# First three experts fixed, the third's gate and up weights loaded early, and the first expert's later passes in short pieces

## What is computed

```python
scores = jax.nn.sigmoid((h @ router_w).astype(jnp.float32))
sel = scores + router_b.astype(jnp.float32)
...                                  # best group of 4 experts, then the 2 best experts in it
hg = jnp.einsum('td,edf->tef', h, w_gate)        # 16 experts, 1024 x 512 each
hu = jnp.einsum('td,edf->tef', h, w_up)          # 1024 x 512 each
act = jax.nn.silu(hg) * hu * gates[..., None].astype(h.dtype)
return jnp.einsum('tef,efd->td', act, w_down)    # 512 x 1024 each
```

## Time and profile before

| | us |
|---|---|
| median of 3 runs | 544.79 (542.86 to 548.34) |
| the profiled execution, whole | 543.45 |
| its span in the trace | 541.7 |
| PE busy in the span | 474.9 (88%) |
| DVE busy | 232.3 (43%) |
| ACT busy | 147.1 (27%) |
| moved by DMA | 164.64 MB, mean 304 GB/s |

### The profile page before, as it was taken

One profiled execution on the slowest core, in us unless ns is written; L12 is line 12 of the kernel. 1 busy time (PEld: TensorE's weight loads), 2 busy tenths in 40 slices (PEclk: granted clock), 3 DMA queues, 4 the chain that ended last, 5 costly groups with the idle time before them and its releaser, 6 DMA issues. The chain is left out here.

```text
span 541.7 us, 8954 instructions
## 1 busy us (share of the span) xinstructions
PE 474.9 (88%) x3266; PEld 231.1 (43%) x3267; DVE 232.3 (43%) x589; ACT 147.1 (27%) x289; POOL 104.2 (19%) x187
## 2 busy tenths in 40 slices
PE   2569988999979999995897998999999999989893
PEld 1126678655568644572343332333323333323331
DVE  2959976999934401868662101111111101111045
ACT  3555882632148510141121110100110001010052
POOL 3000522988950304400400000000000000000400
PEclk9969999799989999995998999999999999999997
DMA  8992045629497999210797999999999999999922
GB/s 281 420 332 100 16 169 188 238 94 353 140 391 288 377 370 416 93 70 1 277 363 295 413 422 419 416 418 419 418 421 420 418 418 419 418 417 423 399 88 116
DMA packets 42571, 164.64 MB, mean 304 GB/s; under 512 B 3314, under 2 KB 4106, under 8 KB 32676
## 3 DMA queue, kind: packets, MB, share of 16 engines
q1 hardware_dynamic: 35440, 144.22, 67.5%
q10 hardware_dynamic: 4580, 11.91, 5.8%
q0 software_dynamic: 2512, 7.99, 4.0%
HBM read 152.77 MB, written 11.34 MB: 303 GB/s over the span
## 5 line engine op out<-in xcount | busy, mean ns | idle before, releaser
L763 PE MATMUL psum<-arena 128*64 128x512 f32 x672 | 150.7, 600 | 17.0 <-DVE arena L1668 7.8
L763 PEld LDWEIGHTS psum<-arena 128*64 128x64 f32 x672 | 49.6, 138 | 104.2 <-issue 102.1
L776 PE MATMUL psum<-arena 128*64 128x512 f32 x336 | 75.9, 592 | 0.0
L1673 DVE TENSOR_TENSOR arena<-arena,psum 128x256 f32<-128x256 f32 x21 | 8.8, 421 | 143.3 <-ACT arena L1119 143.0
L1928 POOL DMA_INDIRECT arena<-sorted_outputs,src_u x6 | 5.7, 951 | 243.5 <-DMA sorted_outputs<-arena 242.0
L776 PEld LDWEIGHTS psum<-arena 128*64 128x64 f32 x336 | 25.6, 137 | 46.1 <-issue 46.1
L1119 ACT ACTIVATE arena<-psum 128x256 f32<-128x256 f32 x21 | 8.0, 383 | 130.8 <-PE psum L763 115.3
L673 PE MATMUL psum<-arena 128*128 128x512 f32 x96 | 42.2, 594 | 0.0
L1134 ACT ACTIVATE arena<-psum 128x512 f32<-128x512 f32 x19 | 11.3, 597 | 57.9 <-PE psum L776 57.9
L673 PEld LDWEIGHTS psum<-arena 128*128 128x128 f32 x96 | 17.9, 190 | 21.2 <-issue 20.9
L1668 DVE COPY arena<-arena 128x512 f32 x31 | 13.1, 422 | 30.4 <-issue 30.4
(11 more groups left out here) (355 smaller groups left out, 646.6 us busy)
## 6 DMA issues: line engine op xcount, KB each, us to landing
arena<-in_w_gate SPq DMA_DIRECT2D x32, 1024.0 KB, 16.0
arena<-in_w_up SPq DMA_DIRECT2D x32, 1024.0 KB, 18.4
arena<-in_w_down SPq DMA_DIRECT2D x16, 2048.0 KB, 15.5
arena<-in_w_mod SPq DMA_DIRECT2D x12, 2048.0 KB, 12.7
arena<-in_w_in SPq DMA_DIRECT2D x3, 2048.0 KB, 21.6
sorted_outputs<-arena ACTq DMA_DIRECT2D x38, 128.0 KB, 6.4
arena<-in_w_out SPq DMA_DIRECT2D x2, 2048.0 KB, 19.0
arena<-modulation_rows ACTq DMA_DIRECT2D x4, 1024.0 KB, 10.6
```

What stands on the lines that cost most here:

```text
L763: last = mm(bank[0][HALF * t:HALF * t + HALF, :], xs[:, side, k, :], gu[:, :, k, t * 256:t * 256 + 256], start=(k == 0), stop=(k == KD - 1))
L776: last = mm(bank[4][HALF * h:HALF * h + HALF, :], hiddenT[:, s * P + t * HALF:s * P + t * HALF + HALF], dn[:, 2 * t + s, h * 512:h * 512 + ...
```

## The change

The first three experts to run become 0, 4 and 8 (`EARLY`), whatever their counts, and the third's gate and up are loaded early, as soon as the output projection's last matmuls are done (`wo_ready` 6). For that the third set moves (gate and up in slots 7 and 8, down in slot 6), and the sorted tiles go where `h2` and `first_rows` were; tile 5 shares its place with tile 0 and is loaded after tile 0 is transposed. The fourth expert's gate and up are issued as soon as expert 0's gate products are done, ahead of the third's down. Expert 0's second pass is cut up: its gate and up, then one sorted tile, then its down and transposes, then the other tiles; the last down product of expert 0 and the first gate and up of the second expert now stand ahead of the loop, and the loop is turned by one expert (4 rounds, and two experts behind it). If expert 0 has over 128 tokens, all six passes run. The key of the running order is changed for the experts behind the first three: with rank r, it is r + 1.75 where r is under 9.5, and 0.5 r from there on, ascending.

```diff
+EARLY = (0, 4, 8)
-        hsr = view(slot(7), 6, D)
+        hsr = [view(at, D) for at in (slot(6), slot(6) + 1024, slot(6) + 2048, slot(6) + 3072, F + 12544, slot(6))]
-            b = (3, 0, 6)[j]
-            return view(slot(b), 2, KD, DE), view(slot(b + 2), 4, D)
+            gu, dn = ((3, 5), (0, 2), (7, 6))[j]
+            return view(slot(gu), 2, KD, DE), view(slot(dn), 4, D)
...
+            sp.wait_ge(S("wo_ready"), 6)
+            load_gate_up(2, EARLY[2])
             sp.wait_ge(S("tok_sent"), 16 * 6)
-            for t in range(6):
-                sp.dma_start(hsr[:, t, :], hsd[t * P:(t + 1) * P, :]).then_inc(S(f"hs_in{t}"), 16)
-            sp.wait_ge(S("first_ready"), 1)
+            sp.wait_ge(S("pad_sent"), 48)
+            sp.wait_ge(S("first_ready"), 4)
+            for t in (0, 1, 2):
+                load_sorted(t)
+            load_sorted(4)
             sp.wait_ge(S("onehots_done"), 1)
-            sp.wait_ge(S("pad_sent"), 48)
             sp.wait_ge(S("int_done"), 1)
-            third = expert_at(2)
...                                  # its two gate halves (L428)
+            load_sorted(3)
+            fourth = expert_at(SETS)
+            sp.wait_ge(S("hs_ready"), 2)
+            load_sorted(5)
+            sp.wait_ge(S("gated"), PASSES)
+            load_gate_up(0, fourth)
             sp.wait_ge(S("hs_ready"), 12)
...                                  # its two up halves (L432)
-            load_down(2, third)
-            for e in range(SETS, NE):
+            load_down(2, EARLY[2])
+            sp.wait_ge(S("downed"), PASSES + 1)
+            load_down(0, fourth)
+            for e in range(SETS + 1, NE):
                 reload(e % SETS, e)
...                                  # PE
             with pe.If(first_n > HALF):
-                second_pass(0, 0, 0)
-            for t in range(6):
+                gate_up(0, turn(1, 0), None, 1)
+                with pe.If(first_n < P + 1):
+                    pe.wait_ge(S("gated"), turn(2, 0))
+                    pe.sem_inc(S("gated"), PASSES - 2)
+            sorted_columns(0)
+            with pe.If(first_n > HALF):
+                down(0, 1, turn(1, 0), turn(0, 0))
+                transposes(turn(1, 0))
...                                  # "crossed" and "downed" counted up, or skipped(0, 1)
+            for t in range(1, 6):
                 sorted_columns(t)
+            with pe.If(first_n > P):
...                                  # passes 2 to 5 in a loop
+            down(0, 1, turn(PASSES, 0), turn(PASSES - 1, 0))
             pe.wait_ge(S("hs_copied_a"), 6)
             pe.wait_ge(S("hs_copied_v"), 6)
...
+            gate_up(1, turn(0, 1), 1)
+            transposes(turn(0, 1))
+            expert_rest(1, 1, 0)
+            with pe.Fori(0, 4) as i:
+                for j in (2, 0, 1):
+                    e = i * SETS + 2 + (j + 1) % SETS
+                    use = i + (j < 2)
+                    first_pass(j, e, use)
+                    expert_rest(j, e, use)
...                                  # DVE: order of the experts
-            v(ts(turn_key, rank, 0.15, None, ALU.mult))
-            for r in (2.0, 4.0):
-                v(stt(turn_key, rank, r, turn_key, ALU.is_equal, ALU.add))
+            v(ts(counted_rank, rank, 0.5, 1.75, ALU.mult, ALU.add))
+            v(stt(counted_rank, rank, 9.5, counted_rank, ALU.is_lt, ALU.mult))
+            v(stt(turn_key, rank, 0.5, counted_rank, ALU.mult, ALU.add))
...                                  # DVE: last_i of expert 0, one operation ahead of int_done
+            v(stt(r2[:, 0, 0:1], r2[:, 1, 0:1], PASSES - 1.0, r2[:, 0, 0:1], ALU.mult, ALU.max))
...                                  # DVE: staging of the second expert, ahead of the loop
+            second = dve.value_load(off_i[0:1, 1:2], min_val=0, max_val=PAIRS)
+            stage_x(second)
+            stage_x(second + HALF, 1)
+            multiply(turn(0, 1))
+            expert_rest(1)
```

More of the change, by code:

```diff
@@ L747, in sorted_columns @@
                         last = tr(bank[SORT_BANK[t][h]][:, kk * P:(kk + 1) * P],
[L748 removed]
+                                  hsr[t].rearrange("p (q k) -> p k q", k=KD)[:, k, :], ident[:, :])
                     last.then_inc(S("hs_ready"), 1)
@@ new lines, in _ @@
+            with pe.Else():
+                skipped(0, 1)
+            for t in range(1, 6):
+                sorted_columns(t)
+            with pe.If(first_n > P):
+                pe.wait_ge(S("hs_copied_a"), 6)
+                pe.wait_ge(S("hs_copied_v"), 6)
+                with pe.Fori(2, PASSES) as q:
+                    gate_up(0, q + turn(0, 0), None)
+                    down(0, 1, q + turn(0, 0), q + turn(0, 0) + -1)
+                    transposes(q + turn(0, 0))
+            down(0, 1, turn(PASSES, 0), turn(PASSES - 1, 0))
@@ L855, in _, with first_pass @@
             pe.wait_ge(S("hs_copied_a"), 6)
             pe.wait_ge(S("hs_copied_v"), 6)
-            with pe.If(first_n > HALF):
-                later_passes(0, 0, 0, first_n)
-            with pe.Else():
-                skipped(0, 1)
-            with pe.Fori(0, 5) as i:
-                for j in range(SETS):
-                    e = i * SETS + j
-                    use = i + (j + 1) // SETS
-                    gate_up((j + 1) % SETS, turn(0, e + 1), use + 1)
-                    down(j, i + 1, turn(PASSES, e), turn(PASSES - 1, e))
-                    transposes(turn(0, e + 1))
-                    expert_rest((j + 1) % SETS, e + 1, use)
+            def first_pass(j, e, use):
+                gate_up(j, turn(0, e), use + 1)
+                down((j + 2) % SETS, use + (j + 2) // SETS, turn(PASSES, e + -1), turn(PASSES - 1, e + -1))
+                transposes(turn(0, e))
@@ new lines, in _ @@
+            gate_up(1, turn(0, 1), 1)
[7 more added lines that the diff above has]
+                    expert_rest(j, e, use)
+            for e in (PREV, LAST):
+                first_pass(e % SETS, e, e // SETS)
+                expert_rest(e % SETS, e, e // SETS)
@@ L1188, in _ @@
             with act.If(first_n > HALF):
-                later_passes(0, 0, first_n)
+                with act.If(first_n > P):
+                    for q in range(2, PASSES):
+                        gate(turn(q, 0))
+                        evacuate(2 - (q - 1) % 2, turn(q, 0), turn(q - 1, 0), (q - 1) * HALF)
+                with act.Else():
+                    skipped(0, 2)
             with act.Else():
                 skipped(0, 1)
+            last_pass(0, 0)
+            gate(turn(0, 1))
+            expert_rest(1, 1)
             with act.Fori(0, 6) as i:
-                for y in range(2):
-                    gate(turn(0, i * 2 + y + 1))
-                    last_pass(i * 2 + y, y)
-                    expert_rest(i * 2 + y + 1, 1 - y)
-            gate(turn(0, PREV - 1))
-            last_pass(PREV - 2, 0)
-            expert_rest(PREV - 1, 1)
+                for y in (1, 0):
+                    e = i * 2 + (2 - y)
+                    gate(turn(0, e + 1))
+                    last_pass(e, y)
+                    expert_rest(e + 1, 1 - y)
             gate(turn(0, PREV))
@@ L1572, in _ @@
             d(V_.memset(before[:, 2 * NE:2 * NE + 1], 0.0))
-            d(V_.memset(prio[:, 0:1], 65536.0))
-            d(V_.memset(prio[:, 1:2], 32768.0))
             dve.wait_ge(S("tri_done"), 1)
-            d(cp(prio[:, 2:NE], desc[:, 2:NE]))
+            for i, e in enumerate(EARLY):
+                d(V_.memset(prio[:, e:e + 1], 65536.0 / 2 ** i))
+                d(cp(prio[:, e + 1:(*EARLY, NE)[i + 1]], desc[:, e + 1:(*EARLY, NE)[i + 1]]))
             dve.wait_ge(S("tri_done"), 4)
```

54 lines of the change are left out of this document (33 added, 21 removed).

## The result

| | before | after |
|---|---|---|
| median, us | 543.83 (542.52 to 548.34, 4 runs) | 556.86 (554.87 to 557.18, 4 runs) |
| ratio after to before | | 1.0217, 95% interval 1.0151 to 1.0283 |
| the profiled execution, its span | 543.45, 541.7 | 554.87, 553.1 |
| PE busy | 474.9 (88%) | 476.8 (86%) |
| DMA, mean GB/s | 304 | 298 |

The change costs 13 us where 5 were forecast, and 556.86 lies outside the range of 543.5 to 555.0. PE's busy time grew by 1.9 us only, in the same 3266 instructions: the rest of the loss is idle time.

A forecast was written before the change was run, and what follows sets the result against it. The prediction took the weight stream as the bound, barely ahead of PE. Weights landing 3.4 us later plus 1.6 us of clock gave +5.0, span 546.7; adding the profiled run's span-to-median difference gave 549.8 us, range 543.5 to 555.0.

The forecast's parts named there:

- What bounds the kernel: From 290 to 504 us: weight stream sets the end, barely; gaining alone is worth about 1.2 us, losing costs all.
- The early load: Third expert's 4 MiB behind the last output projection: done by 248 us, costs nothing, later stream 10.0 us shorter.
- Place 0 in pieces: First expert's cut-up second pass on PE: nothing won ahead of the loop, 0.7 us lost.
- ACT's skip: Before place 0's last down product, PE waits for ACT to skip unused passes: 1.2 us, between 0.66 and 2.11.
- G(1): Start of the second-run expert's first gate-and-up multiply: 293.3 us against 290.14; W + n counts from the output projection's end.
- rival C: Ahead of the third-run expert: the pieces pay on PE, its first multiply starting at 301, not 304; -3.0 us, chance 0.12.
- The jumps: Branches on PE around place 0: 0.3 us each; loop steps afterwards kept from the kernel before, 11.54 us per one-pass place.
- G(4): Start of the fifth-run expert's first gate-and-up multiply, behind the three-pass expert: 349.0 us, with place 6's weights issued at 348.3.
- Rival E: Around place 0: costlier turnovers or one instruction-loading stall; +3.0 to +3.3 us more, 553 us, chance 0.20.
- The hole: Before place 6's weights: three-pass expert at place 3 holds their set, leaving the stream empty some 12 us.
- The stream behind the hole: From place 6 on: landings 15.85 us apart, the last interval 18.3; place 15's weights land at 507.3, 3.4 later.
- The clock: In the last multiply: a 3.9 us wait on weights lowers PE's clock, costing 1.6 us.

The follow-up runs named there:

- The first two rows of the table: The change itself, ratio 1.0217 to the kernel before; and the change with the tensor engine's branch behind place 1's first pass left out, ratio 1.0198.
- the kernel without stalls: The change in its own order, with the tensor engine's jumps behind the first passes of places 1, 14 and 15 left out: 547.2 us, ratio 1.0076.
- the square of the two causes: The change with its order or the three-pass expert at place 8, each with jumps kept or out at places 1, 14, 15: 1.0217, 1.0129, 1.0076, 0.9934.

## Why the prediction was wrong

In the order of its steps:

**What bounds the kernel: right.** PE and the stream run level, and a stream that loses costs it all. The first two rows of the table, where 9.9 us won by PE at G(5) gave 1 us of total by the ratios and 3 by the medians, bear it out.

**The early load: right.** Issued at 232.60, right behind the output projection; its last w_up piece landed 11.9 us after its issue at 233.92, at 245.8, against "by 248". It disturbed nothing there. With the holes behind it, it was worth 3 us of 10, which is within the spread.

**Place 0 in pieces: near.** ACT's skip was taken at 1.2 us and cost nothing: the down product ran at 285.20, right behind the sorted transposes. So G(1) came at W + 56.1, forecast W + 57.9. In the kernels without place 1's jump the stage behind it has an idle of 1.83, and G(2) comes 41.5 to 41.7 us behind the first gate and up of place 0, where the kernel before has 43.1 and the forecast 43.8 (G(2) at W + 66.3 or W + 68.0, by where place 0 started). So rival C (the pieces pay 3 us on PE) was nearly right, 2.3 us of its 3, once the jump behind place 1 was gone; in the change that jump took more than this back.

**The jumps: the step that failed.** The jumps inside place 0, for which the sum had 0.3 each, were near: PE stood idle for 0.15 us ahead of tile 0's transposes, not at all ahead of the down product, and for 0.59 us ahead of the other tiles. What failed are two terms behind them. For G(2) the sum has DVE's 2.1 and 0.43 and "PE 0.1 later", and nothing for PE's own jump behind place 1. From G(2) on it carries over the steps of the kernel before (11.54 for a place of one pass, with a turnover of 0.66), in which no jump of the loop happened to stall. In the change the jumps behind places 1 and 4 took 5.6 and 3.7 us of PE's sequencer, and 2.0 and 1.5 us of clock behind them (9.07 and 8.56 against 7.09). G(4) came at W + 117.7 instead of W + 113.6, and so did the issue that ends the hole: W + 117.0, where W + 112.9 was forecast and the kernel without stalls has W + 112.3. Rival E named the kind ("one stall of instruction loading", 553), at 0.20 and one stall; there were two. Its evidence was in the page of the profile, a queue of instruction loads with 24 packets. Its size of 3.3 us came from the tail's step, which no run shows to be a load of code: in the trace of before no instruction packet falls into 509 to 517.

**The hole: right in place and in what ends it, shorter than forecast.** Issue of place 6 at G(4) - 0.8, forecast G(4) - 0.7; its last piece landed 13.3 us later, forecast 13.2. (The Trainium skill's estimate from "DMA: Bandwidth & Descriptors", section "Anatomy of one DMA", by which this landing would come 1.0 sooner, did not hold here; that section is on transfers that GpSimd issues, and these are SP's.) Between the last landing and that issue the queue held no weights for 7.8 us (341.75 to 349.54), and for 6.8 us in the same order without stalls. The forecast's "some 12 us" doesn't follow from its own times either, 338 and 348.3. The sum goes by the end of the hole, so its length cost the forecast nothing. The view of the w_up pieces issued at 349.97 and 350.96 has it:

```profile
DMA to landing us min/median/max: 7.8/9.9/11.9
```

**The stream behind the hole: sized too small, and made up elsewhere.** From landing(6) to landing(15) the forecast has 0.7 + 8 x 15.85 + 18.3 = 145.8. The kernel in the change's order without stalls took 149.7: 17.6 for the first interval, 15.6 to 16.2 for the next seven, and 21.2 for the last. The change took 151.2, with 17.4, 16.9, 16.5 and 17.4 for the first four, at 383, 415, 376 and 406 GB/s: in three of them the queue ran low. The interval of 15.85 from the earlier trace rows holds for a full queue only. The last interval was not slower but had more to move: 8.86 MB in 21.2 us against 7.66 MB in 18.3 us in the kernel before, both at 418 to 419 GB/s. When the stream is late, traffic of the kernel's end (the gathers of the results among it) falls ahead of its last landing; 1.2 MB more are 2.9 us.

**The clock: near.** 1.6 us was taken behind a wait near 4 us; it was 2.4 behind 4.44 (6.01 against 3.65).

Put together from the profile: landing(15) came at W + 281.5 instead of W + 271.9 (+9.6; 4.2 of it at landing(6), 5.4 behind it), the clock took 0.8 more, the rest of the tail 1.2 less (36.6 against 37.8). That is +9.2 over the forecast, 320.5 against 311.3. Without stalls the profile (of its fastest run) has 311.8, and the median is 0.8% over before, 4.1 us [2.3, 5.9], where 5.0 was forecast. That agreement is partly luck: landings 3.3 later, no clock price on the half that counts (1.6), and 1.2 less of tail. (Most of the 1.2 are idle times of PE in the tail of before: 0.68 and 0.79 us in two places, where this kernel has 0.40 and nothing.)

**Still open.** Where exactly each jump lies against what PE has loaded no view shows: that position decides is shown by the sixty-four instructions, the loads by the packets, and the link between the two is inferred. Whether a full DMA queue makes such a load longer wasn't tested. The worth of the change's good parts, with order and stalls put right, is 2.1 us for early load and late order (542.17 against 544.27, beside each other) and 0.0036, 2 us, for the pieces and the moved product. Their intervals overlap, and only their sum against the kernel before is clear of no change.

## What to carry to other kernels

Where a queue of weights runs ahead of the compute, ask of every place that holds a buffer longer how much is queued at that moment: the same three-pass expert was free at place 7 or 8 and cost 7.7 us at place 3 (5 to 11 by the stalls that stood beside it). When code is added, moved or peeled from a loop, or other jumps are taken in it, allow for a stall of some 3 to 6 us at one or two of the jumps that are taken for the first time on a busy engine, look in the new trace for idle times released by the engine's own sequencer, and don't judge the idea before these are away: two versions of one idea may differ by 1% through code position alone. A change that is an improvement in two parts and a mistake in a third shows as a loss; the square of the two causes, four kernels, told more than any single undoing.

## What the runs showed of the hardware that was not expected

- A jump taken for the first time on PE: an idle of 0.4 to 1.1 us ahead of the next matmul where it doesn't stall, and of 2.6 to 7.1 us where it does (2.64, 2.86, 4.32, 4.48, 4.53, 4.71, 4.76, 5.08, 6.11, 6.17, 6.29 and 7.13 among others, in nine kernels), with a packet of 0.02 MB on the queue of instruction loads some 3 to 4 us before PE goes on, where that was looked up us by us. No jump that had been taken before stalls in any of the traces, and most first ones don't either.
- One jump that was taken out removed two stalls, and made a third at another place. 64 instructions at the start of the program moved them too.
- The granted clock falls to the 1.2 GHz level behind most such idles (0.55 in the mean from 300 to 305 in the change), and a multiply of 7.09 then takes 8.6 to 10.2: 9.07 behind 6.17, 10.01 behind 5.08, 10.23 behind 5.93, 8.64 behind 4.76. An idle of 1.83 cost nothing in three kernels, nor did 2.86 in another, and 1.84 in a fifth cost 1.7 (8.78). The Trainium skill ("TensorE: Matmul & The Clock Gate", section "What's actually happening") has the same two levels; the loss doesn't grow evenly with the idle time in these rows.
